# One of four convolution blocks on GpSimd and the causal mask as a matmul, in a two-layer encoder trunk

## The reference, cut to what matters

```python
def stick_breaking_attention(q, k, v):
    ...
        z = jnp.einsum('bhqd,bhkd->bhqk', q_blk, k).astype(jnp.float32) * scale
        causal = key_pos[None, :] < t[:, None]
        log_fail = jnp.where(causal, jax.nn.log_sigmoid(-z), 0.0)
        tail = lax.cumsum(log_fail, axis=3, reverse=True) - log_fail
        a = jnp.where(causal, jnp.exp(jax.nn.log_sigmoid(z) + tail), 0.0)
        return jnp.einsum('bhqk,bhkd->bhqd', a.astype(v.dtype), v)

def conformer_conv(u, b_glu, dw, dw_b, ln_g, ln_b):
    u = u + b_glu
    a, g = jnp.split(u, 2, axis=-1)
    h = a * jax.nn.sigmoid(g)
    h = causal depthwise convolution of h with the 31 taps dw, + dw_b
    mu, var = mean and variance of h over the 512 channels
    return jax.nn.silu((h - mu) * lax.rsqrt(var + EPS) * ln_g + ln_b)

def even_mixer(...):
    ...
    return jnp.concatenate([a_out, b_out], axis=-1) @ w_out
```

## Time and profile before

| what | us |
|---|---|
| median of 3 runs | 1314.75 (1313.68 to 1317.06) |
| the profiled execution's own time | 1314.29 |
| its span in the trace | 1312.5 |
| PE busy | 905.3 (69%) |
| DVE busy | 334.9 (26%) |
| ACT busy | 176.0 (13%) |
| POOL busy | 35.1 (3%) |
| data moved | 490.10 MB, 373 GB/s over the span |

### The profile page before, as it was taken

One profiled execution on the slowest core, in us unless ns is written; L12 is line 12 of the kernel. 1 busy time (PEld: TensorE's weight loads), 2 busy tenths in 40 slices (PEclk: granted clock), 3 DMA queues, 4 the chain that ended last, 5 costly groups with the idle time before them and its releaser, 6 DMA issues.

```text
span 1312.5 us, 14970 instructions
## 1 busy us (share of the span) xinstructions
PE 905.3 (69%) x6198; PEld 426.3 (32%) x6198; DVE 334.9 (26%) x889; ACT 176.0 (13%) x415; POOL 35.1 (3%) x75
## 2 busy tenths in 40 slices
PE   4898698575556557466779999885656557466557
PEld 2765444221212122121248745441212122121212
DVE  1278535111121111111231135541121111111122
ACT  1013322000000000000113235410000000000000
POOL 1000110000000000000000000200000000000000
PEclk8998898887787787786889999997787777787779
DMA  9978618999999999999999449399999999999996
GB/s 338 390 260 320 249 68 363 429 429 424 429 428 426 429 429 426 431 425 429 410 408 392 155 159 369 137 383 427 428 428 427 428 427 429 428 427 428 428 424 270
DMA packets 64172, 490.10 MB, mean 373 GB/s; under 512 B 11489, under 2 KB 11634, under 8 KB 41586
## 3 DMA queue, kind: packets, MB, share of 16 engines
q1 hardware_dynamic: 58048, 486.62, 89.2%
q10 hardware_dynamic: 6066, 2.64, 0.7%
HBM read 488.20 MB, written 1.05 MB: 373 GB/s over the span
## 4 chain that ended last, share of the span: by engine, by line
DMA 49%; PE 34%; DVE 7%; SPq 3%; ACTq 2%; ACT 2%; issue 2%; POOL 0%; DVEq 0%
PE psum L1306 33%; DMA weight_ring<-in_moe_w_down 16%; DMA weight_ring<-in_moe_w_up 15%; DMA weight_ring<-in_moe_w_gate 15%; DVE phase_region L955 4%; ACTq L580 2%; DMA weight_ring<-in_w_ada 2%; SPq L406 2%; SPq L460 1%; ACT h_or_mix_T L615 1%; PE psum L1353 0%; ACT phase_region L604 0%; DVE phase_region L887 0%; SPq L415 0%; DVE x_tokens L909 0%
## 5 line engine op out<-in xcount | busy, mean ns | idle before, releaser
L1306 PE MATMUL psum<-weight_ring,phase_region 128*32 128x512 f32 (+1 forms) x3456 | 455.3, 688 | 344.4 <-DMA weight_ring<-in_moe_w_gate 146.8
L1306 PEld LDWEIGHTS psum<-weight_ring,phase_region 128*32 128x32 f32 x3456 | 132.9, 129 | 651.8 <-issue 625.6
L1306 PE MATMUL psum<-phase_region 128*128 128x128 bf16 (+4 forms) x1168 | 144.1, 286 | 4.2 <-DVE x_tokens L1119 1.7
L1306 PE MATMUL psum<-h_or_mix_T,weight_ring 128*128 128x256 f32 (+1 forms) x520 | 116.9, 384 | 8.0 <-ACT h_or_mix_T L615 8.0
L1306 PEld LDWEIGHTS psum<-phase_region 128*128 128x128 bf16 (+3 forms) x1168 | 87.5, 120 | 78.7 <-issue 58.2
L1306 PEld LDWEIGHTS psum<-h_or_mix_T,weight_ring 128*128 128x128 f32 x520 | 99.8, 195 | 23.2 <-DVE h_or_mix_T L896 5.4
L1306 PE MATMUL psum<-weight_ring,h_or_mix_T 128*128 128x512 f32 x224 | 101.4, 604 | 3.4 <-DVE scale L872 3.4
L1172 DVE TENSOR_TENSOR phase_region<-psum,gate_rows 128x512 f32<-128x512 f32 x32 | 22.1, 692 | 217.3 <-PE psum L1306 217.3
L754 ACT ACTIVATE phase_region<-psum 128x512 f32<-128x512 f32 x16 | 9.6, 597 | 486.0 <-PE psum L1306 486.0
L1160 DVE SCALAR_TENSOR_TENSOR phase_region<-phase_region,psum 128x512 f32<-128x512 f32 x16 | 11.0, 688 | 248.2 <-ACT phase_region L754 248.2
L1165 DVE SCALAR_TENSOR_TENSOR phase_region<-phase_region,psum 128x512 f32<-128x512 f32 x16 | 16.9, 1056 | 222.4 <-PE psum L1306 222.4
(11 more groups left out here) (175 smaller groups left out, 464.2 us busy)
## 6 DMA issues: line engine op xcount, KB each, us to landing
weight_ring<-in_moe_w_gate SPq DMA_DIRECT2D x64, 2048.0 KB, 19.9
weight_ring<-in_moe_w_up SPq DMA_DIRECT2D x64, 2048.0 KB, 20.1
weight_ring<-in_moe_w_down SPq DMA_DIRECT2D x64, 2048.0 KB, 19.9
weight_ring<-in_w_ada SPq DMA_DIRECT2D x12, 3072.0 KB, 16.4
weight_ring<-in_w_ada SPq DMA_DIRECT2D x12, 1024.0 KB, 18.6
weight_ring<-in_odd_w_in SPq DMA_DIRECT2D x6, 2048.0 KB, 24.3
weight_ring<-in_even_w_in SPq DMA_DIRECT2D x4, 2048.0 KB, 24.7
weight_ring<-in_even_w_out SPq DMA_DIRECT2D x2, 2048.0 KB, 11.4
```

Source lines behind the costliest of these rows:

```text
L1306: return pe.matmul(out_, lhsT, rhs, start=first, stop=last, **kw)
```

## The change

It does four things to layer 0's mixer.

1. GpSimd no longer masks. It takes block 3 of the convolution (`CONVD`): for each tap a `tensor_scalar` into `TAPPED`, then a `tensor_tensor` add into `CACC`, 61 instructions of 256 columns in all, each add waiting for its product. VectorE keeps blocks 0 to 2 (93 instructions instead of 124).
2. The causal mask is added to the logits by TensorE: for each head and each diagonal block one more 128x128 product of `BIGID` (2^100 on the diagonal) with `NEGTRI`, four per pair. `tails` and `values` then wait for VectorE and ScalarE directly.
3. All 31 taps run before the first `soft_plus`. The channel sums stand ahead of `tails(0)` and behind `tails(1)`; centring, squares, scaling and sigmoid stand ahead of pairs 2 and 3.
4. The output projection starts with the convolution's blocks; unit 0 uses PSUM bank 6 instead of 4, and it waits for `take_modulation(2)`. The modulation sums (3), the join of the gate and sums (4) lie later.

```diff
...
+            link(g.memset(BIGID[:, :], 0.0))
+            link(g.affine_select(out=BIGID[:, :], in_=BIGID[:, :], compare_op=ALU.not_equal, fill=BIG, base=0,
+                                 pattern=[[-1, P]], channel_multiplier=1))
             g.memset(GL8[:, :, :], LOWEST).then_inc(consts_ready, 1)
-            def keep_past(tile, i, ready, done):
...
-                keep_past(PRe, i, probs_exp, probs_masked)
+            pool.wait_ge(cols_ready, 2)
+            pool.wait_ge(glu_ready, 1)
+            for j in range(TAPS):
+                src = CIN[:, CONVD, j:j + S]
+                tap = CV1[:, j * CB + CONVD:j * CB + CONVD + 1]
+                if j == 0:
+                    g.tensor_scalar(CACC[:, CONVD, :], src, tap, CV2[:, 8 + CONVD:9 + CONVD], ALU.mult, ALU.add).then_inc(conv_pool, 1)
+                    continue
+                if j > 2:
+                    pool.wait_ge(conv_pool, j - 2)
+                g.tensor_scalar(TAPPED[:, j % 2, :], src, tap, None, ALU.mult).then_inc(conv_tapped, 1)
+                pool.wait_ge(conv_tapped, j)
+                pool.wait_ge(conv_pool, j)
+                ins = g.tensor_tensor(CACC[:, CONVD, :], CACC[:, CONVD, :], TAPPED[:, j % 2, :], ALU.add)
+                ins.then_inc(conv_pool, 1)
...
                 act.wait_ge(pv_done, i + 1)
                 a.copy(HT[:, i, :], PS[:, 7, 0:S]).then_inc(heads_out, 1)
+            def probabilities(i):
+                act.wait_ge(logs_min, i + 1)
+                v = PRe[:, i % 2, :, :]
+                a.activation(v, v, ACT.Exp).then_inc(probs_exp, 1)
             soft_logs(0)
             soft_logs(1)
             copy_partials(2)
-            for i in range(NPAIR):
...
-            take_heads(NPAIR - 1)
+            act.wait_ge(conv_centred, 1)
+            a.activation(CSQ[:, :, :], CACC[:, :, :], ACT.Square).then_inc(conv_squared, 1)
+            probabilities(0)
+            probabilities(1)
+            act.wait_ge(conv_var, 1)
+            link(a.activation(RSTD[:, :], PS[:, 6, S:2 * S], ACT.Ln, scale=1.0 / CONV, bias=EPSC[:, 0:1]))
+            a.activation(RSTD[:, :], RSTD[:, :], ACT.Exp, scale=-0.5).then_inc(conv_rstd, 1)
+            soft_logs(2)
+            act.wait_ge(conv_floor, 1)
+            sigmoid(CSQ[:, :, :], conv_exp)
+            take_heads(0)
+            soft_logs(3)
+            take_heads(1)
+            for i in range(2, NPAIR):
+                probabilities(i)
+            for i in range(2, NPAIR):
+                take_heads(i)
...
             def glu():
                 dve.wait_ge(glu_exp, 1)
-                link(v.tensor_tensor(CIN[:, :, PAD:PAD + S], CIN[:, :, PAD:PAD + S], CACC[:, :, :], ALU.mult))
+                v.tensor_tensor(CIN[:, :, PAD:PAD + S], CIN[:, :, PAD:PAD + S], CACC[:, :, :], ALU.mult).then_inc(glu_ready, 1)
+                dve.wait_ge(glu_ready, 1)
             def conv_taps(lo, hi):
                 for j in range(lo, hi):
-                    for b in range(CB):
+                    for b in range(CONVD):
                         src = CIN[:, b, j:j + S]
                         tap = CV1[:, j * CB + b:j * CB + b + 1]
                         if j == 0:
                             ins = v.tensor_scalar(CACC[:, b, :], src, tap, CV2[:, 8 + b:9 + b], ALU.mult, ALU.add)
                         else:
-                            dve.wait_ge(conv_done, CB * (j - 1) + b + 1)
+                            dve.wait_ge(conv_done, CONVD * (j - 1) + b + 1)
                             ins = v.scalar_tensor_tensor(out=CACC[:, b, :], in0=src, scalar=tap, in1=CACC[:, b, :],
                                                          op0=ALU.mult, op1=ALU.add)
                         ins.then_inc(conv_done, 1)
...
                 v.scalar_tensor_tensor(out=s, in0=PS[:, b:b + 2, 0:3 * P], scalar=0.0, in1=s,
                                        op0=ALU.max, op1=ALU.add).then_inc(fail_sum_in, 1)
-            glu()
...
-            for i in range(NPAIR):
+            def floor_logs(i):
                 dve.wait_ge(logs_ready, i + 1)
                 if i >= 2:
                     dve.wait_ge(pv_done, i - 1)
                 b = 2 * (i % 2)
                 v.tensor_scalar(PRe[:, i % 2, :, :], PS[:, b:b + 2, 0:3 * P], 0.0, None, ALU.min).then_inc(logs_min, 1)
-                if i == 0:
...
-                    take_modulation(3)
+            glu()
+            conv_taps(0, TAPS)
+            soft_plus(0)
+            soft_plus(1)
+            dve.wait_ge(conv_mean, 1)
+            for b in range(CB):
+                ins = v.scalar_tensor_tensor(out=CACC[:, b, :], in0=PS[:, 6, 0:S], scalar=-1.0 / CONV,
+                                             in1=CACC[:, b, :], op0=ALU.mult, op1=ALU.add)
+            ins.then_inc(conv_centred, 1)
+            floor_logs(0)
+            floor_logs(1)
+            dve.wait_ge(conv_rstd, 1)
+            for b in range(CB):
+                ins = v.scalar_tensor_tensor(out=CACC[:, b, :], in0=CACC[:, b, :], scalar=CV2[:, 12 + b:13 + b],
+                                             in1=RSTD[:, :], op0=ALU.mult, op1=ALU.mult)
+            link(ins)
+            for b in range(CB):
+                ins = v.tensor_scalar(CSQ[:, b, :], CACC[:, b, :], CV2[:, 16 + b:17 + b], SIGMOID_FLOOR,
+                                      ALU.add, ALU.max)
+            ins.then_inc(conv_floor, 1)
+            soft_plus(2)
+            soft_plus(3)
+            dve.wait_ge(conv_exp, 1)
+            for b in range(CB):
+                ins = v.scalar_tensor_tensor(out=HT[:, NPAIR + b, :], in0=CACC[:, b, :],
+                                             scalar=CV2[:, 16 + b:17 + b], in1=CSQ[:, b, :],
+                                             op0=ALU.add, op1=ALU.mult)
+            ins.then_inc(conv_out, 1)
+            take_modulation(2)
+            floor_logs(2)
+            take_modulation(3)
+            floor_logs(3)
+            take_modulation(4)
             dve.wait_ge(consts_ready, 1)
             link(v.scalar_tensor_tensor(out=NDIST[:, :], in0=NDIST[:, :], scalar=-1.0, in1=NDIST[:, :],
...
                 if (L, 0) not in mixed:
                     slab_ready(slab)
                     rest_ready(slab)
-                    pe.wait_ge(ada_ready, 6 * L + 5)
+                    pe.wait_ge(ada_ready, (3, 11)[L])
                 done = mixed.setdefault((L, u), set())
                 for k in blocks:
-                    ins = mm(PS[:, mixed_banks[u], :], HT[:, k, t * P:(t + 1) * P], wide(slab)[:, k, h * HALF:(h + 1) * HALF],
+                    ins = mm(PS[:, mixed_banks[L][u], :], HT[:, k, t * P:(t + 1) * P], wide(slab)[:, k, h * HALF:(h + 1) * HALF],
                              not done, len(done) == KD - 1, skip_group_check=True)
                     done.add(k)
                 if len(done) == KD:
...
                     r = slice(h * HD, (h + 1) * HD)
                     b = 2 * (i % 2) + h
                     mm(PS[:, b, 0:S], KTe[r, i, 0:P], QTe[r, i, :], True, True)
-                    ins = mm(PS[:, b, S:S + P], KTe[r, i, P:S], QTe[r, i, P:S], False, True, skip_group_check=True)
+                    mm(PS[:, b, S:S + P], KTe[r, i, P:S], QTe[r, i, P:S], False, True, skip_group_check=True)
+                for h in range(2):
+                    b = 2 * (i % 2) + h
+                    for at in (0, S):
+                        ins = mm(PS[:, b, at:at + P], BIGID[:, :], NEGTRI[:, :], False, True, skip_group_check=True)
                 ins.then_inc(z_ready, 1)
             def tails(i):
-                pe.wait_ge(fails_masked, 4 * (i + 1))
+                pe.wait_ge(fail_sum_in, i + 1)
                 for h in range(2):
                     b = 2 * (i % 2) + h
                     s = SPe[:, i % 2, h, :]
...
                 ins.then_inc(logs_ready, 1)
             def values(i):
-                pe.wait_ge(probs_masked, 4 * (i + 1))
+                pe.wait_ge(probs_exp, i + 1)
                 if i:
                     pe.wait_ge(heads_out, i)
                 for h in range(2):
...
                     ins = mm(PS[:, 6, at:at + S], ONES[:, :], tile[:, b, :], b == 0, b == CB - 1, skip_group_check=True)
                 return ins
-            for i in range(NPAIR):
...
-            pe.wait_ge(heads_out, NPAIR - 1)
+            pe.wait_ge(conv_done, TAPS * CONVD)
+            pe.wait_ge(conv_pool, TAPS)
+            channel_sum(CACC, 0).then_inc(conv_mean, 1)
+            tails(0)
+            tails(1)
+            pe.wait_ge(conv_squared, 1)
+            channel_sum(CSQ, S).then_inc(conv_var, 1)
+            values(0)
+            logits(2)
+            modulation_sums(3)
+            values(1)
+            logits(3)
+            pe.wait_ge(conv_rstd, 1)
+            gate_join(2)
+            tails(2)
+            pe.wait_ge(conv_out, 1)
+            mix_out(0, 0, (4, 5, 6, 7))
+            tails(3)
+            values(2)
+            modulation_sums(4)
+            pe.wait_ge(ada_ready, 4)
```

(48 more changed lines are left out.)

69 lines of the change are left out of this document (7 added, 62 removed).

## The result

| what | us |
|---|---|
| the kernel before, median of 5 runs | 1314.75 (1313.68 to 1317.06) |
| the changed kernel, median of 5 runs | 1326.77 (1324.39 to 1329.98) |
| ratio, 95% interval | 1.0085 [1.0073, 1.0098] |
| profiled execution, its span | 1329.13, 1327.1 |

The change makes the kernel 0.85% slower by the ratio, about 11 us; the two medians of the table lie 12.0 us apart. The forecast of 1319 had the sign and less than half of the size (4.9 us), and 1326.77 lies outside its range of 1304 to 1325.

The account below looks back on a forecast made before the run. The mixer's chain, not the weight stream, was taken to set this stage, passing shifts on nearly one for one. Unit 1's delay 2.4, later DVE operations 0.6 and a clock fall 1.9 made +4.9 on 1314.3: 1319 us, range 1304 to 1325.

Parts of the forecast that it names:

- What bounds the kernel: Weight stream bounds the whole span, but has no slack after this mixer; its shift reaches the kernel nearly one for one.
- Unit 1: Output projection unit whose end the prediction counts by: 183.4 us against 181.0, before additions of 0.6 and 1.9.
- That the engines hinder each other: In the convolution, DVE taps reading two SBUF tensors and GpSimd instructions reading SBUF take turns throughout.
- The rows of the masks: Old trace: four GpSimd masks took 1.03 us usually, 1.21 and 1.62 beside DVE instructions reading two SBUF tensors.
- The price of a turn: Convolution, priced by reading time: a GpSimd tap takes 1.30 us, DVE doing two taps instead of three; ends at 128.5.
- GpSimd's prices: Convolution block on GpSimd: product 0.39 us, add 0.62, a tap 1.1; 31 taps unhindered end near 109.
- rival 1: Convolution: engines hinder each other little or not; channel sum starts at 116, kernel 1305.6 or 1303.7 us; chance 13%.
- Rival 3: Convolution: whole instructions exclude each other, or GpSimd's tap operand costs more; taps end at 145, kernel 1336; chance 15%.
- halfway point: Kernel time of 1327 us, given as halfway within Rival 3, whose full case is 1336.
- The two new waits: TensorE waits 2.4 us before values(1) for the head copy and 2.9 us before the first output piece.
- The clock behind them: Each new TensorE wait may drop its clock; one fall counted, 3.65 - 1.74 = +1.9 us.
- one stretch of 55.4 us: From last tap to unit 1's end, 55.4 us against 45.5, because mixing work now stands behind the taps.

Follow-up runs that it names:

- e3: The changed kernel with VectorE's running convolution sums in PSUM, only the last tap written to SBUF: 1323.65 us, ratio 1.0054 to the kernel before.
- e5: The changed kernel with GpSimd's product written with a second operation that changes nothing (plus 0.0): 1326.77 us, ratio 1.0092 to the kernel before.
- e2: The changed kernel with VectorE starting its taps only when GpSimd has ended its own: 1355.98 us (one run).
- e6: The changed kernel with GpSimd's two-operation product and VectorE's running sums in PSUM: 1308.38 us, ratio 0.9941 to the kernel before.
- e1: The changed kernel with all four convolution blocks on VectorE and GpSimd idle in the mixer: 1320.44 us, ratio 1.0039 to the kernel before.
- e7: e6 plus two exchanges: head copy ahead of ScalarE's soft_logs(2), convolution output ahead of VectorE's soft_plus(3): 1301.51 us, ratio 0.9892 to the kernel before.
- e9: The kernel before with only the causal mask moved to TensorE, old order, convolution all on VectorE: 1312.18 us, ratio 0.9968 to the kernel before.
- e8: e1 plus both order exchanges of e7, convolution all on VectorE: 1311.67 us, ratio 0.9969 to the kernel before.
- e4: e1 with VectorE's running sums in PSUM, GpSimd idle: 1319.94 us, ratio 1.0032 to the kernel before.
- e10: e6 plus only the first exchange, ScalarE's head copy ahead of soft_logs(2): 1301.27 us, ratio 0.9894 to the kernel before.

## Why the prediction was right or wrong

- **What bounds the kernel: right.** Unit 1 moved by 12.2 us, the weight transfer behind it by 12.2, the median by 12.0. No transfer took up any of it. The profiled execution as a whole came out 14.6 us longer (1327.1 against 1312.5), so in that one some 2.4 us lie behind this stage.
- **That the engines hinder each other: right**, and e3 shows the cause. The rows of the masks were enough to see it. That DVE pays too was harder to read there: the 1.80 us of L994 are 1.67 in the changed kernel, where no GpSimd instruction runs beside it, but L1004's 1.69 are 1.66.
- **The price of a turn: this is the step that failed.** It said "1.30 us, in which DVE does two taps instead of three", a loss of 0.51 us per step, 15.3 in all, because some 0.12 us at the start and the end of each instruction would overlap with the other engine. Measured: 0.47 for the add and 0.22 for the product, 0.69 per step, 20.7 in all. In its own terms, it gave a GpSimd step 0.27 + 0.49 = 0.76 us of reading and let 0.25 of them cost DVE nothing; 0.69 of them cost it. The difference is 5.4 us, and the taps ended 5.5 later than 128. (Two small things cancel: the taps began 0.6 earlier than assumed, and the sum gave 128.5 where 128 was taken.) e5 shows it purest: two DVE taps in a step of 1.485, not 1.30.
- **GpSimd's prices: wrong, and here without effect.** The product was put at 0.39, in part from a two-operation row of 384 columns whose factor is a constant; unhindered it takes 0.92 as written (e2) and 0.48 with two operations (e6). The add was put at 0.62 and takes 0.73. In the change this costs nothing (e5), since DVE ends last either way. In e3 it is the bound: rival 1's condition, taps ended before about 123, could not be met with this product even without any hindrance, so rival 1 was worth less than its 13%.
- **Rival 3, whole instructions: not so.** At the prediction's prices the taps would end at 145. At those measured alone it would be 75.9 + 93 x 0.397 + 30 x (0.92 + 0.73) = 162 (an estimate from e1 and e2); they ended at 133.5. e5 speaks against it too, since halving the product's length changed nothing for DVE. By the Trainium skill (SBUF — State Buffer, "SBUF: two separate sides") whichever starts first gets the shared pair for its whole instruction; the traces don't agree on this. That 1326.77 lies at this rival's halfway point, 1327, is luck: the product was indeed dearer than thought, but e5 shows that this cost nothing here.
- **The two new waits: right** in place and size, 2.54 and 3.19 us against 2.4 and 2.9. **The clock behind them: half right.** One fall of 1.9 us was counted; both waits had one, 2.54 + 1.92 against 1.74 + 1.16 and 5.31 against 3.67, together 3.2. Tails behind the channel sum were slow for a part too, 4.88 against 3.63 at full clock (e7). With the waits this makes taps' end to unit 1 59.7 us, where 57.9 was forecast.
- **Not priced: the order by itself.** The prediction took mask and order as one stretch of 55.4 us against 45.5 and did not ask what each was worth. e9 and e1 say that the mask helps by 4 and the order loses 9.

In sum: unit 1 at 185.9 forecast, 193.2 measured; 5.5 of the 7.3 are the turns, 1.8 the clock and the waits.

## What to carry to other kernels

Before a share of a chain of DVE instructions goes to GpSimd, count their SBUF operands: with two, each GpSimd instruction that ran beside them here cost DVE 0.2 to 0.5 us, and a product of half the length as much as the whole one; with one operand in PSUM, at the same price per instruction, nothing. When work is gathered so that all of it waits for one event, look at what each engine has queued behind that event: moving one copy of 0.4 us ahead of ScalarE's logarithms and sigmoid was worth 5.6 us in the trace. And take a large edit apart before judging it: of three parts here one helped, two hurt, and both that hurt could be mended, after which the block on GpSimd was worth about 10 us (e8 to e7).

## What the runs showed of the hardware that was not expected

- On GpSimd, `tensor_scalar` of 128x256 fp32 with a per-partition operand took 0.92 us with one operation (e2, alone) and 0.48 with two (e6, beside DVE taps with their sum in PSUM). Why is open; other shapes were not tried.
- Beside GpSimd, DVE taps with both tensors in SBUF took up to 0.95 us each, against 0.47 unhindered; with the sum in PSUM each took 0.48, one every 0.39, and GpSimd was not slowed either (e3).
- The two engines fell into step: DVE did a whole number of taps per GpSimd step, three in 1.88 us (the change) and two in 1.485 (e5), in every step. With the sum in PSUM they did not: four or five taps in 1.71 us (e3).
- The same wait of TensorE was followed by a lower clock in some kernels and not in others. Behind 2.54 us the granted clock fell to 1.2 GHz for a part of the next work in the change, in e1, e3 and e4 (`values` took 2.5 to 3.1 us), not in e2, e5 and e6 (1.74); behind 3.19 it fell in all seven of these, in which the wait of 2.54 stands ahead of it (the output piece took 5.3 to 6.7 us), and not in e10 (3.67), where that one is gone. The length of the wait alone doesn't decide it, and what does was not settled.
